# Modulation rows by plain fp32 matmuls on unsplit blocks, spread over the first layer

## The chip, the cores and the metric

One core of one Trainium2 chip runs the whole program. The metric is the device time of one execution in microseconds, the median of several runs. Work on the core is shared by TensorE (PE, matmuls; PEld is its weight load), VectorE (DVE), ScalarE (ACT), GpSimd (POOL) and SyncE (SP); in this kernel SP only issues weight loads and POOL mostly issues the small transfers.

## The reference, cut to what matters

A two-layer diffusion backbone on 128 context and 256 latent tokens, model width 1024, all in fp32. Every sub-block is steered by "adaLN" rows, which come from one vector-matrix product per layer and conditioning vector:

```python
def _adaln(cvec, w, b):
    m = (jax.nn.silu(cvec) @ w + b).reshape(-1, 1, 6 * D_MODEL)
    return jnp.split(m, 6, axis=-1)
...
mp = _adaln(c_ctx, mod_w[i], mod_b[i])
ms = _adaln(c, mod_w[i], mod_b[i])
hp = _modulate(_rmsnorm(xp, norm1_g[i]), mp[0], mp[1])   # shift, scale
... # attention || retention, output projection
xp = xp + mp[2] * op                                      # gate
hp = _modulate(_rmsnorm(xp, norm2_g[i]), mp[3], mp[4])
... # dense SwiGLU (layer 0) or top-2-of-8 experts (layer 1)
xp = xp + mp[5] * fp
```

`mod_w` is 2 x 1024 x 6144 in fp32, 50 MB, multiplied by two vectors only. Layer 0 has a combined input projection (1024 to 2816), windowed attention beside chunkwise retention, an output projection and a SwiGLU; layer 1 has a neighbourhood attention and the experts.

## The kernel before, in words

All large products are made at near-fp32 accuracy out of three fp32r matmuls. A weight block of 128 x 1024 fp32 (512 KB) is loaded by SP into one of `RAW = 6` buffers `rawb`. ACT copies it to `whi` (rounded to fp32r, `conv_hi`, L467), DVE computes `wlo = raw - whi` (`conv_lo`, L472), both in `HL = 3` slots, and TensorE multiplies high by high, high by low and low by high (`mm3`, L522, L525, L526). The blocks of all dense stages have one running number b. SP may reload the raw buffer of b once `lo_done` counts its conversion; ACT may overwrite the slot of b once `pe_used` counts the matmuls of b - 3. The helper `Ahead` lets ACT and DVE convert up to three blocks ahead of TensorE.

The modulation rows go the same way. The two conditioning vectors, after silu and split in high and low, are four stationary columns `cs4` (padded to 128), and each mod block is 2 x 128 rows by 512 columns, moving in four matmuls (L1318 and L1320 in a loop for layer 0, L880 and L882 in `mod1` for layer 1). Twelve chunks of four blocks make the 6144 columns of one layer. Results, four rows of 512, are copied by ACT to `mst` or `mst1` (L1690, L1443), stored by POOL to a scratch in DRAM (L724, L712), and loaded back as rows of `mrow` (`norm_mods`, L718). There DVE multiplies the scale rows by the norm's weight (`scale_rows`, L1760), ACT and DVE split `mrow` into high and low (`split_rows`, L1418, L1764), and TensorE broadcasts the rows to 128 partitions by a matmul with a selector matrix `sel_r` (`rows_bc`, L829; `norm_bc`, and `norm_gate` for the gates). DVE applies them to x (L1778, L1784), TensorE transposes the result (`turn_in`, L861), ACT and DVE split it into `hT_hi` and `hT_lo` (L1424, L1792).

Order of the work, the same on every engine: all 48 mod blocks of layer 0; 8 mod blocks of layer 1; norm 0; the input projection, 22 blocks, with two mod blocks of layer 1 behind each of the first 20 (`MOD_PER`, `mod_behind`); retention, whose matmuls are small plain fp32 ones in eight steps j (L1024, L1036, L1051, L1058, L1059); attention of layer 0 in 24 units n of one head and one token tile (scores L954, transposes L964, values L986, preparation of keys and queries per pair of heads in `prep`, L926 and L933); output projection (8 blocks); norm 1; SwiGLU; norm 2; layer 1's projection, attention, output; norm 3; the experts. Each engine's program is written out by hand, and semaphores tie them together.

In the experts, tokens beyond 128 of one expert are computed from the raw blocks in plain fp32: `oF` and `oT` are 128 x 32 stationary tiles, and four column groups of 32 output rows each take a quarter of the columns (L1235, L1254).

## Time and profile before

| | |
|---|---|
| runs of the kernel before | 2031.91, 2034.63, 2095.38 us, median 2034.63 |
| profiled execution | 2029.53 us, its span 2027.9 us |
| mean granted TensorE clock | 0.915 of full speed |
| busy TensorE | 1842.5 us (91%), 9817 matmul records |
| busy VectorE | 1291.8 us (64%) |
| busy ScalarE | 1088.9 us (54%) |
| moved by DMA | 416.61 MB, mean 205 GB/s |

The page cuts the span into 40 slices of 50.7 us. The first six, in which the mod blocks are loaded, run at 174 to 331 GB/s; the granted clock is near half in slices 7 and 8 (retention and attention of layer 0). A matmul's busy time overlaps that of its neighbour, because it is pipelined, so the distance between the starts of two matmuls tells more than the duration of one. A plain fp32 matmul leaves two records in this trace, an fp32r matmul or a transpose one.

### The profile page before, as it was taken

To read this page: it belongs to the slowest core of one execution; us is meant where nothing else is said; L and a number is where in the kernel's file an instruction comes from. 1 tells how busy PE (TensorE), PEld (TensorE's weight loads), DVE (VectorE), ACT (ScalarE), POOL (GpSimd) and SP (SyncE) were. 2 spreads that over 40 slices of the span, in tenths; PEclk is the share of its full clock that TensorE was granted. 3 is DMA by queue.
4 is the path that set the end of the run, shared out by engine and by line. 5 is a ranking of instruction groups with operands and counts; after the bars stand their busy time and mean duration, and the time that the engine had idled before them with its cause. 6 is when DMAs were issued, how large, how long until landed. Compare 5 with 4: busy or idle time off the path is not lost.

```text
span 2027.9 us, 27794 instructions
## 1 busy us (share of the span) xinstructions
PE 1842.5 (91%) x9817; PEld 1453.8 (72%) x9818; DVE 1291.8 (64%) x1599; ACT 1088.9 (54%) x1493; POOL 154.4 (8%) x225
## 2 busy tenths in 40 slices
PE   4868889999999999999869989999999999999992
PEld 2546677677888877867657868877877777778781
DVE  3764565554434344356537647679898989898985
ACT  3755552433333233356316546567777777777771
POOL 3010010000000004043020000000000000000001
PEclk7879995588999998999859989999999999999996
DMA  8956650022444435422315766789999999999971
GB/s 273 331 174 223 226 184 11 0 86 83 124 124 125 125 107 143 125 68 49 115 53 202 256 245 219 253 314 337 337 337 327 338 325 334 340 334 325 339 267 37
DMA packets 199740, 416.61 MB, mean 205 GB/s; under 512 B 17436, under 2 KB 36948, under 8 KB 199632
## 3 DMA queue, kind: packets, MB, share of 16 engines
q1 hardware_dynamic: 188928, 394.31, 56.8%
q0 software_dynamic: 10704, 20.86, 3.7%
q8 instruction: 67, 1.10, 0.2%
q14 instruction: 41, 0.34, 0.0%
HBM read 415.00 MB, written 5.90 MB: 208 GB/s over the span
## 4 chain that ended last, share of the span: by engine, by line
PE 76%; DVE 11%; ACT 5%; issue 3%; DMA 3%; POOL 0%; SPq 0%; ACTq 0%; DVEq 0%; POOLq 0%
PE ps L522 20%; PE ps L526 19%; PE ps L525 19%; PE ps L954 3%; DVE wlo L495 3%; DMA rawb<-in_mod_w 2%; PE ps L1235 2%; ACT whi L467 2%; PE ps L986 2%; DVE wlo L472 2%; PE ps L964 2%; ACT whi L491 2%; PE ps L1183 1%; PE ps L1254 1%; DVE h L1778 1%
## 5 line engine op out<-in xcount | busy, mean ns | idle before, releaser
L472 DVE TENSOR_TENSOR wlo<-rawb,whi 128x1024 fp32r<-128x1024 f32 x224 | 271.9, 1234 | 344.1 <-ACT whi L467 342.9
L467 ACT ACTIVATE whi<-rawb 128x1024 fp32r<-128x1024 f32 x224 | 231.8, 1055 | 352.2 <-PE ps L526 319.3
L495 DVE TENSOR_TENSOR wlo<-rawb,whi 128x1024 fp32r<-128x1024 f32 x288 | 349.0, 1223 | 111.2 <-ACT whi L491 107.9
L491 ACT ACTIVATE whi<-rawb 128x1024 fp32r<-128x1024 f32 x288 | 304.6, 1060 | 141.1 <-PE ps L526 140.4
L495 DVE TENSOR_TENSOR wlo<-rawx,whi 128x1024 fp32r<-128x1024 f32 x240 | 291.1, 1223 | 56.7 <-ACT whi L491 53.1
L491 ACT ACTIVATE whi<-rawx 128x1024 fp32r<-128x1024 f32 x240 | 254.7, 1061 | 112.8 <-PE ps L526 111.9
L522 PE MATMUL ps<-whi,eT_hi 128*128 128x512 f32 (+1 forms) x768 | 301.7, 393 | 3.8 <-DVE wlo L495 1.9
L525 PE MATMUL ps<-wlo,eT_hi 128*128 128x512 f32 (+1 forms) x768 | 291.1, 379 | 0.0
L526 PE MATMUL ps<-whi,eT_lo 128*128 128x512 f32 (+1 forms) x768 | 291.1, 379 | 0.0
L522 PE MATMUL ps<-whi,hT_hi 128*128 128x512 f32 (+1 forms) x672 | 261.1, 388 | 20.9 <-DVE wlo L472 17.1
L525 PE MATMUL ps<-wlo,hT_hi 128*128 128x512 f32 (+1 forms) x672 | 256.8, 382 | 0.0
L526 PE MATMUL ps<-whi,hT_lo 128*128 128x512 f32 (+1 forms) x672 | 256.7, 382 | 0.0
L522 PEld LDWEIGHTS ps<-whi,eT_hi 128*128 128x128 f32 x768 | 149.1, 194 | 51.2 <-DVE wlo L495 23.8
L526 PEld LDWEIGHTS ps<-whi,eT_lo 128*128 128x128 f32 x768 | 148.9, 194 | 27.2
L522 PEld LDWEIGHTS ps<-whi,hT_hi 128*128 128x128 f32 x672 | 128.2, 191 | 54.8 <-DVE wlo L472 24.6
L525 PEld LDWEIGHTS ps<-wlo,eT_hi 128*128 128x128 f32 x768 | 149.5, 195 | 22.0
L526 PEld LDWEIGHTS ps<-whi,hT_lo 128*128 128x128 f32 x672 | 128.2, 191 | 24.7
L525 PEld LDWEIGHTS ps<-wlo,hT_hi 128*128 128x128 f32 x672 | 128.4, 191 | 22.9
L522 PE MATMUL ps<-whi,eF_hi 128*128 128x512 f32 x352 | 143.7, 408 | 0.0
L526 PE MATMUL ps<-whi,eF_lo 128*128 128x512 f32 x352 | 139.0, 395 | 0.0
L525 PE MATMUL ps<-wlo,eF_hi 128*128 128x512 f32 x352 | 138.8, 394 | 0.0
L522 PEld LDWEIGHTS ps<-whi,eF_hi 128*128 128x128 f32 x352 | 66.2, 188 | 21.7 <-issue 4.5
(311 smaller groups left out, 2430.9 us busy)
## 6 DMA issues: line engine op xcount, KB each, us to landing
rawb<-in_od_moe_w_gu SPq DMA_DIRECT2D x192, 512.0 KB, 5.4
rawx<-in_od_moe_w_gu SPq DMA_DIRECT2D x160, 512.0 KB, 5.3
rawb<-in_mod_w SPq DMA_DIRECT2D x96, 512.0 KB, 5.2
rawb<-in_od_moe_w_down SPq DMA_DIRECT2D x96, 512.0 KB, 5.1
rawx<-in_od_moe_w_down SPq DMA_DIRECT2D x80, 512.0 KB, 5.4
rawb<-in_ev_ffn_w_gu SPq DMA_DIRECT2D x44, 512.0 KB, 3.7
rawb<-in_od_w_qkv SPq DMA_DIRECT2D x24, 512.0 KB, 3.6
rawb<-in_ev_w_in SPq DMA_DIRECT2D x22, 512.0 KB, 3.8
```

The source lines that it names most:

```text
L467: nc.scalar.activation(whi[:, r, :], rawb[:, s, :], ACT.Copy).then_inc(hi_done, 1)
L472: nc.vector.tensor_tensor(wlo[:, r, :], rawb[:, s, :], whi[:, r, :].bitcast(F32), ALU.subtract).then_inc(lo_done, 1)
L491: nc.scalar.activation(whi[:, moe_slot(i), :], moe_raw(j), ACT.Copy).then_inc(hi_done, 1)
L495: nc.vector.tensor_tensor(wlo[:, moe_slot(i), :], moe_raw(i % EB), whi[:, moe_slot(i), :].bitcast(F32), ALU.subtract).then_inc(lo_done, 1)
L522: first_mm = nc.tensor.matmul(out, l_hi, r_hi, start=start, stop=False)
L525: nc.tensor.matmul(out, l_hi, r_lo, start=False, stop=False)
L526: return nc.tensor.matmul(out, l_lo, r_hi, start=False, stop=stop)
L954: nc.tensor.matmul(ps[:, g % 2, 0:hi - lo], qT[r, i % 2, t * P:(t + 1) * P], kT[r, sl, lo:hi], start=True, stop=True).then_inc(at_s, 1)
L964: mm = nc.tensor.transpose(ps[:, 2 + g % 2, c * P:(c + 1) * P], s_p[:, g % 2, c * P:(c + 1) * P], ident)
L986: mm = nc.tensor.matmul(ps[:, 6 + m % 2, DH * u:DH * (u + 1)], s_pT[:, g % 2, c * P:(c + 1) * P], v, start=(c == 0), stop=(c == len(vs) - 1))
L1183: mm = nc.tensor.transpose(ps[:, 6 + s % 2, c * P:(c + 1) * P], eg[:, c * P:(c + 1) * P], ident)
L1235: mm = nc.tensor.matmul(ps[q * OV:(q + 1) * OV, 2 + g, 0:P], oT[:, k, :], moe_raw(j0 + k // rows)[:, c:c + P], start=(k == 0), stop=(k == ...
```

## The change

The modulation product is done without splitting. The two vectors, silu applied, stand in `csz`, 128 x 32 per k, columns 2 to 31 zero, plain fp32. A mod block j is now 128 rows (one k) by the 1024 columns of one of six parts; it is read straight from `rawb` in four fp32 matmuls of 256 columns, each in its own column group of 32 (`mod_mm`). Eight blocks make one of `MODS = 12` parts q. ACT copies a part to `mst` (128 x 256, `mod_take`), POOL stores it and later loads two rows of each group back into `mrow`.

Only parts 0 and 1 (shift and scale of layer 0's first norm) are computed ahead of norm 0. Parts 2 to 5 go behind the first 16 blocks of the input projection, two blocks each; part 6 into retention, one block behind each step; parts 7 to 11 into attention of layer 0, two blocks behind each of 20 units. The gate of layer 0's first sub-block is therefore broadcast during the output projection (`gate_first`), not in norm 0. SP's loads follow one list `SEQ` of mod and weight blocks; a raw buffer is free again when `mod_used` (mod blocks) or `lo_done` (weights) counts it. `whi` and `wlo` hold weight blocks only. Layer 0's `prep` uses one PSUM bank for keys and queries, as bank 4 now takes mod parts 6 to 11. The statistics of norm 0 are computed before the mod parts are taken.

```diff
+MODS, MOD_PER = 12, 2
+B_OUT0 = IN_BLOCKS
+MOD_AFTER = {}
+for _j in range(2 * KD, 6 * KD):
+    MOD_AFTER.setdefault((_j - 2 * KD) // MOD_PER, []).append(_j)
+SEQ = [("m", _j) for _j in range(2 * KD)] + [("w", _b) for _b in range(HL)]
+for _b in range(IN_BLOCKS - HL):
+    SEQ += [("w", _b + HL)] + [("m", _j) for _j in MOD_AFTER.get(_b, ())]
+SEQ += [("m", _j) for _j in range(6 * KD, 7 * KD)] + [("w", B_OUT0 + _b) for _b in range(HL)]
+SEQ += [("m", _j) for _j in range(7 * KD, MODS * KD)] + [("w", _b) for _b in range(B_OUT0 + HL, B_MOE)]
+MOD_IN_ATT = {n: (7 * KD + 2 * i, 7 * KD + 2 * i + 1) for i, n in
+              enumerate(n for s in range(2, 23, 5) for n in range(s, s + 4))}
...
+            for p, (kind, i) in enumerate(SEQ):
+                if p >= RAW:
+                    was, n = SEQ[p - RAW]
+                    sp.wait_ge(*((mod_used, n + 1) if was == "m" else (lo_done, n + 1 + RAW)))
...
+            def mod_store(q):
+                pool.wait_ge(mod_ev, q + 1)
+                if q:
+                    pool.wait_ge(mod_out, 16 * q)
+                pool.dma_start(mods[q], mst[:, q % 2, :]).then_inc(mod_out, 16)
...
+            def gate_first(b):
+                kind = b - B_OUT0
+                if kind not in (0, 1):
+                    return
+                if kind:
+                    pe.wait_ge(gate_ev, 1)
+                else:
+                    pe.wait_ge(mr_l, 2)
+                for half in range(2):
+                    mm = rows_bc(6 + half, 64, 4 + kind, half, 7)
+                mm.then_inc(gate_ps, 1)
...
-            def mod1(b):
-                c, i = b // SB, b % SB
-                pe.wait_ge(lo_done, N_MOD1[b] + 1 + RAW)
...
-                for kk in range(2):
-                    k = 2 * i + kk
-                    nc.tensor.matmul(ps[:, mod_bank(c), :], cs4[:, 4 * k:4 * k + P], wblk(whi, N_MOD1[b], 512)[:, kk, :],
-                                     start=(k == 0), stop=False)
-                    mm = nc.tensor.matmul(ps[:, mod_bank(c), :], cs4[:, 4 * k:4 * k + P],
-                                          wblk(wlo, N_MOD1[b], 512)[:, kk, :], start=False, stop=(k == KD - 1))
-                mm.then_inc(pe_used, 1)
+            def mod_mm(j):
+                q, k = divmod(j, KD)
+                if k == 0 and q == 6:
+                    pe.wait_ge(up_ev, 1)
+                elif k == 0 and q > 3:
+                    pe.wait_ge(mod_ev, q if q > 6 else q - 1)
+                pe.wait_ge(*landed("m", j))
+                for g in range(4):
+                    mm = nc.tensor.matmul(ps[32 * g:32 * (g + 1), mod_bank(q), 0:2 * P], csz[:, k, :],
+                                          rawb[:, slot_at("m", j), g * 2 * P:(g + 1) * 2 * P], start=(k == 0),
+                                          stop=(k == KD - 1))
+                mm.then_inc(mod_used, 1)
...
             def prep(lay, i):
-                kb, qb = (6, 7) if lay and i == 0 else (4, 5)
+                kb, qb = (6, 7) if lay and i == 0 else (4, 5) if lay else (5, 5)
+                if not lay:
+                    if i:
+                        pe.wait_ge(at_qT, i)
+                    else:
+                        pe.wait_ge(gn_c, 1)
...
+                    if lay == 0:
+                        pe.wait_ge(at_kT, ki + 1)
...
+                    if lay == 0:
+                        for j in MOD_IN_ATT.get(n, ()):
+                            mod_mm(j)
...
+            def mod_take(q):
+                act.wait_ge(mod_used, KD * (q + 1))
+                if q > 1:
+                    act.wait_ge(mod_out, 16 * (q - 1))
+                nc.scalar.activation(mst[:, q % 2, :], ps[:, mod_bank(q), 0:2 * P], ACT.Copy).then_inc(mod_ev, 1)
...
+            norm_stats(0)
+            for q in range(2):
+                mod_take(q)
             split_rows(0)
-            norm(0, 0)
-            dense(IN_CH, 0, proj0, tables)
+            ahead = Ahead(act, conv_hi, 0)
+            ahead.to(HL)
+            turn_in(0)
+            dense(IN_CH, 0, proj0, tables, limit=B_OUT0)
```

## Rows read from the trace of the kernel before

**Rows 1.** The page: engines on the chain that ended last; GB/s of its slices
```profile
PE 76%; DVE 11%; ACT 5%; issue 3%; DMA 3%; POOL 0%; SPq 0%; ACTq 0%; DVEq 0%; POOLq 0%
GB/s 273 331 174 223 226 184 11 0 86 83 124 124 125 125 107 143 125 68 49 115 53 202 256 245 219 253 314 337 337 337 327 338 325 334 340 334 325 339 267 37
```

**Rows 2.** Stages: PE, PEld, DVE, ACT, POOL busy, clock, DMA share, GB/s
```profile
0.00:140.60 140.60, 86.46 (x274) 55.91 (x275) 85.89 (x89) 78.44 (x94) 24.49 (x49) 0.81 0.82 277
140.60:295.00 154.40, 137.23 (x593) 107.30 (x592) 81.38 (x85) 85.16 (x119) 5.19 (x10) 0.98 0.63 205
295.00:338.00 43.00, 39.79 (x259) 34.93 (x259) 16.27 (x37) 9.62 (x20) 3.65 (x6) 0.69 0.08 21
338.00:410.00 72.00, 70.37 (x230) 48.10 (x228) 43.58 (x138) 31.66 (x93) 0.00 (x0) 0.50 0.03 8
...
878.00:959.00 81.00, 78.98 (x472) 56.20 (x472) 52.75 (x139) 55.10 (x160) 38.22 (x47) 1.00 0.22 47
```

**Rows 3.** Instructions in order of time, TensorE, input projection: start, duration, line
```profile
162.93 0.51 PE L522 MATMUL ps<-whi,hT_hi 128*128 128x512 f32 x1 [0.60 <-DVE wlo L472]
...
167.16 0.39 PE L880 MATMUL ps<-whi,cs 128*128 128x512 f32 x1
...
169.88 0.47 PE L522 MATMUL ps<-whi,hT_hi 128*128 128x512 f32 x1 [0.71 <-DVE wlo L472]
```

**Rows 4.** The same view, TensorE in the experts, 1163 to 1167 us
```profile
1163.97 0.40 PE L526 MATMUL ps<-whi,eF_lo 128*128 128x512 f32 x1
1164.30 1.93 PE L1254 MATMUL ps<-rawb,oF 128*32 128x256 f32 x32
1166.16 0.50 PE L522 MATMUL ps<-whi,eF_hi 128*128 128x512 f32 x1
```

**Rows 5.** The chain in order of time, retention and attention: start, us, what
```profile
303.90 0.72 PE ps L1036 x6
...
310.20 0.72 PE ps L1036 x6
...
320.32 1.39 PE ps L1036 x6
...
325.45 1.39 PE ps L1036 x6
...
359.22 1.57 PE ps L954 x2
```

**Rows 6.** In order of time, ACT and POOL, early front
```profile
33.73 1.06 ACT L467 ACTIVATE whi<-rawb 128x1024 fp32r<-128x1024 f32 x1 [0.27 <-DMA rawb<-in_mod_w]
...
33.29 1.51 POOL L704 DMA_DIRECT2D mrow<-in_mod_b  x3
```

**Rows 7.** In order of time, POOL, DVE, ACT, TensorE; one row of DMA issues
```profile
104.36 0.52 POOL L724 DMA_DIRECT2D mods_scratch<-mst  x1 [18.69 <-ACT mst L1690]
108.34 1.54 POOL L718 DMA_DIRECT2D mrow<-mods_scratch  x3 [3.45 <-DMA mods_scratch<-mst]
...
mrow<-mods_scratch POOLq DMA_DIRECT2D x6, 16.0 KB, 3.2
...
119.30 1.22 DVE L1760 TENSOR_TENSOR mrow<-mrow,gbc 6x1024 f32<-6x1024 f32 x1
...
121.09 1.04 ACT L1418 ACTIVATE mr_hi<-mrow 128x1024 fp32r<-128x1024 f32 x1
122.16 1.23 DVE L1764 TENSOR_TENSOR mr_lo<-mrow,mr_hi 128x1024 fp32r<-128x1024 f32 x1 [1.64 <-ACT mr_hi L1418]
...
127.49 1.28 DVE L1778 SCALAR_TENSOR_TENSOR h<-x,st,ps 128x1024 f32<-128x1024 f32 x1
...
138.56 0.79 PE L829 MATMUL ps<-mr_hi,sel_r 6*128 6x512 f32 x1 [1.38 <-DVE hT_lo L1792]
```

**Rows 8.** Stretches around the turn after attention, columns as in rows 2
```profile
410.70:414.10 3.40, 3.40 (x18) 3.40 (x17) 2.01 (x3) 2.19 (x4) 0.00 (x0) 0.50 0.00 0
414.20:417.60 3.40, 1.83 (x11) 1.39 (x10) 3.20 (x4) 1.18 (x3) 0.00 (x0) 1.00 0.00 0
```

## What I predict before the changed kernel is run

> **What bounds the kernel now.** I first read the page. TensorE is 76% of the chain that ended last, and the DMA engines reach at most 340 GB/s in any slice [rows 1]. An average over the whole run says little here, so I cut the run into stages at the first and last matmul of each [rows 2]. The first 140.6 us produce modulation rows and the first normalization: TensorE is busy for 86 us of them and idle for the rest. The input projection takes 154.4 us, with the DMAs at 205 GB/s. Retention takes 43 us, attention of layer 0 takes 72 us at a granted clock of 0.50 (the 1.2 GHz level), and attention of layer 1, which is twice as long (48 units against 24), takes only 81 us at 1.00 (2.4 GHz). Everything after the output projection of layer 0 is untouched by the change.
>
> Inside the projection, TensorE does one w_in block and then two mod blocks. The block that starts at 162.93 runs to 167.16 (4.23 us), the two mod blocks need about 1.9 us, and the next block starts only at 169.88, after a wait for wlo [rows 3]: a period of 6.95 us. The reason is in the code. There are three whi/wlo slots for w and mod blocks alike, so the next w block can be converted only when the previous w block has left its slot, and the two mod matmul groups are shorter than that conversion.
>
> **The price of a new mod block.** The routed layer already has the new form: plain fp32 matmuls, 128 rows by 32 columns, 256 columns moving, four column groups, on raw blocks. Each such matmul leaves two records. Thirty-two records, which are 16 matmuls or four blocks, run from 1164.30 to 1166.16 [rows 4]: 1.86 us, or 0.465 us a block at full clock; at half clock I take twice that, 0.93. Around the group 0.10 us is lost going in (0.33 between starts instead of 0.23) and I take as much coming out. So a pair costs 0.93 + 0.2 = 1.14 us, and a lone block 0.68. Before, a pair of blocks cost 1.9 us on TensorE plus one conversion pass per block on ACT and one on DVE. The lower bound is 0.465 without any switch. The upper bound is four matmuls one after another: the nearest row is a score matmul of 384 columns, 1.57 us at half clock for its two records [rows 5], so 256 columns cost 1.05 us at half clock and 0.52 at full, and a block 2.1 us at full clock. I take the low value, because its row has this very form.
>
> The Trainium skill (TensorEngine Tiling, Key Properties) says that changing the tiling mode drains TensorE. If every one of the 88 switches (16 in the projection, 8 in retention, 20 in attention, in and out) cost a whole 0.39 us matmul over its start distance of 0.23, the sum would be 14 us for switching where the rows above give 9, and the forecast 5 us higher.
>
> **Part 1, the front.** Of 56 mod blocks that ran before the first normalization, 16 stay (shift and scale of layer 0); none is converted. What ends last now is the arrival of these 16. The seventh block was converted at 33.73, already paced by its DMA, and POOL comes to the end of its early queue at 34.8 [rows 6]; both stay. A block is 0.524 MB; at 340 GB/s it takes 1.55 us, but four to six of the later blocks will be in flight or landed by then, since a raw slot is now free as soon as TensorE has read it. I put the sixteenth at 43 us (41 if all of the ring is in by 33; 47.7 if nine blocks follow the seventh one by one). Behind it stands a chain that was hidden by the eight early blocks of layer 1 and is now exposed, its steps taken from [rows 7]: matmuls and the copy to mst 1.2; the store from 104.36 to the issue of the load at 108.34, 4.0; two load issues 1.0 and landing 3.2; scaling 1.22, high part 1.04, low part 1.23 with their hand-overs, 3.7 (the copy of sel moves ahead of the wait). That is 56.1. Then norm: before, the low part ended at 123.39, h began at 127.49 and the last transposed low part released TensorE at 138.56. The statistics are now early, but three conversions stand in DVE's queue ahead of h (last wlo about 3.3 us after the low part), so h begins about 3.5 us after the low part instead of 4.1, and the projection starts at 56.1 + 3.5 + 11.1 = 71, rounded up to 72 for the semaphore delays left out. The gate matmuls (138.56 to 140.6) go to the output projection. The gain is 140.6 - 72 = 68.6 us; bounds 62 to 72.
>
> **Part 2, the projection.** 22 w blocks, 32 mod blocks behind the first 16 of them (before: 40 split ones). The wlo stall goes, because mod blocks no longer take whi/wlo slots: conversion of block b+3 now has two whole blocks of cover. Period 4.1 + 1.14 = 5.25, so 16 x 5.25 + 6 x 4.1 = 108.6, and 2 us for the first blocks at half clock: 111 against 154.4, a gain of 43.4. What is late next is the loads: three blocks (1.57 MB) each 5.25 us are 300 GB/s, under the 340 seen. In the ring of six the load of w(b+5) waits for the conversion of b+3, and the mod loads behind it on SP wait with it; from there (2.3 us of conversion, about 6.7 us to land three, 5.25 us of matmuls) the loop closes in 14.3 us for three periods, 4.8 each, less than 5.25. The margin is small, which is a rival below. The four copies to mst (ACT, 256 columns each) and the stores on POOL lie beside the matmuls.
>
> **Part 3, retention.** One block after each of the eight steps. TensorE hardly waits there, so all of it is on the path: 8 x 0.68 = 5.4 at full clock, 9 at half. A step took 3.15 us at full clock (303.90 to 310.20, two steps) and 5.13 later (320.32 to 325.45, one step) [rows 5]. The dense pieces may keep the clock up for a step or two more, 2 us each. I take +3 (bounds -8, the clock holds throughout, and +9).
>
> **Part 4, attention of layer 0.** Forty blocks in pairs behind 20 of the 24 units. At full clock a unit costs 81/48 = 1.69 us, preparations included; at half clock 72/24 = 3.0 [rows 2]. The preparations now share one PSUM bank and wait for ACT's copy of the keys, twice, and the first one waits for the group norm: +3. The question is the clock. The stage is entered at 0.50 after a DVE-only gap, as before, and the old mix never raised it in 72 us, while layer 1, entered at 1.00, held it with the same mix. Now 1.9 us of full-array work stand in each unit of 4.9 us. The clock rose at about 414 after nothing but transposes back to back [rows 8], so short dense work is enough to raise it. I expect it to rise within about three units: 24 x 1.69 + 20 x 1.14 + 3 + 2 x 1.3 (units before it) + 3 x 2.0 = 75, +3. Loads: 37 blocks x 1.55 = 57 us, covered.
>
> The Trainium skill (TensorE: Matmul & The Clock Gate, Part 4: PE-mode transpose) says that transposes do not count as activity of the engine for the clock. By that rule a third of the attention mix would not help, and the rival at 1960 would be the likelier. The trace speaks against it: 0.50 while only transposes ran, 1.00 right behind them.
>
> **Part 5, turn and output projection.** Of the 24 transposes 18 filled 3.4 us at half clock [rows 8]; at full clock the 4.5 us of all become 2.2: -2.3, say -2.4. Two gate groups of four matmuls at 0.23, +1.9. The rest of these rows (DMAs to mrow, six late stores) is hidden behind 30 us of projection and the norm. -0.5.
>
> **Sum.** -68.6 - 43.4 + 3 + 3 - 0.5 = -106.5, against the profiled execution's 2029.5 (span 2027.9 and 1.6 around it): **1923 us**. The median of the runs is 2034.6, 5 us above; I keep 1923.
>
> **Rivals.**
> (a) *The clock stays at 1.2 GHz through attention.* For: 72 us without a rise. Against: the dense pieces. Then 72 + 40 x 0.93 + 3 = 112 instead of 75, and the transposes stay slow: +39, **1962**. Chance 0.27.
> (b) *The loads become the bound in the projection*: mod blocks sit behind w loads on SP and in the same ring. For: 300 GB/s asked. Against: whole slices ran at 334 to 340 GB/s in the experts, and the loop closes. If the period stays 6.95: 16 x 1.7 = +27, **1950**. Chance 0.10.
> (c) *The column groups do not run side by side* when they stand alone on four new matmuls with a fresh 32-column load: 2.1 us a block, 96 x 1.6 = +154, **2077**, slower than before. It decides from (106.5 / 96) + 0.49, about 1.6 us a block. Against: the rows of the same form. Chance 0.02.
> (d) *The change does not do what it says*, that is, the store and load round trip or POOL's early queue holds the first norm until the old time: all 68 us of the front would be lost, **1991**, about 2% faster. Against: POOL is free at 34.8. Chance 0.02.
> My forecast has the remaining 0.59. Its own range is 1905 to 1942 (front -4/+6, retention -11/+6, attention -5/+8, projection +6).
>
> **Range.** 1903 to 1966 takes in (a) and (b). About 2% (41 us) is what a measurement tells from no change: faster 0.95, same 0.03, slower 0.02.
>
> **What would show it.** First projection matmul near 72; a projection period near 5.25 without waits for wlo; mod groups of 0.47 us a block at 1.00; in attention the granted clock at 1.00 after three or four units; the stage from keys to the last value near 75. A clock of 0.50 throughout means (a), waits for rawb in the projection mean (b), groups of 2 us mean (c).

## The result and the profile after

The changed kernel took 2016.01 us in the median of seven runs (2006.81 to 2023.53). The kernel before, run beside it, took 2037.26 us in the median of seven (2031.91 to 2095.59). The ratio is 0.991, 95% interval 0.988 to 0.994. I had forecast 1923 us, with 1903 to 1966 as the range and 0.95 for a gain of over 2%. It is a gain of about 1%, outside the range.

The cause lies in the spread, so it is told here: the runs of the kernel before stand in two groups, 2028 to 2040 us and 2092 to 2106 us, and the ratio leaves the slower group out.

The page of the changed kernel: the granted clock in 40 slices of 50.3 us, the GB/s of the slices, and the engines on the chain that ended last.

```profile
PEclk7799579799999799555859989999999999999996
GB/s 295 147 288 193 76 248 253 70 126 126 123 124 126 107 139 112 32 11 32 116 54 236 255 217 243 259 312 332 347 337 329 336 327 339 327 331 342 335 264 38
PE 80%; DVE 9%; DMA 4%; ACT 3%; issue 3%; POOL 0%; SPq 0%; DVEq 0%; ACTq 0%; POOLq 0%
```

The clock is low in slices 5 and 6 (retention and attention of layer 0), as it was before a little later. It is also low in slices 17 to 19, at 5, 5 and 5, which hold almost nothing but attention of layer 1. The stages of the changed kernel, columns as in [rows 2]; the rows are the front, the input projection, its end to the first scores, attention of layer 0 up to the first output-projection matmul, from there to the SwiGLU, layer 1's projection, and layer 1's attention up to its output projection:

```profile
0.00:76.30 76.30, 24.24 (x170) 10.82 (x171) 18.43 (x30) 15.27 (x25) 20.60 (x41) 0.66 0.71 238
76.30:191.30 115.00, 113.85 (x688) 83.34 (x688) 33.27 (x43) 39.98 (x69) 4.41 (x8) 0.97 0.70 238
191.30:254.00 62.70, 57.64 (x323) 44.76 (x322) 17.34 (x39) 9.59 (x21) 4.22 (x7) 0.56 0.25 76
254.00:332.40 78.40, 72.04 (x574) 41.57 (x574) 48.49 (x144) 38.48 (x106) 2.72 (x5) 0.85 0.83 296
332.40:387.70 55.30, 49.26 (x200) 37.11 (x200) 32.41 (x37) 20.72 (x27) 3.67 (x7) 0.86 0.28 89
695.10:796.50 101.40, 101.40 (x442) 83.57 (x441) 30.58 (x23) 34.42 (x41) 15.08 (x19) 0.97 0.44 128
796.50:951.80 155.30, 150.99 (x506) 106.39 (x505) 60.74 (x151) 60.31 (x169) 38.35 (x47) 0.52 0.11 27
```

The same last stage in the kernel before, 875.7 to 965.2:

```profile
875.70:965.20 89.50, 83.85 (x506) 59.86 (x505) 57.95 (x151) 60.28 (x169) 38.22 (x47) 1.00 0.21 48
```

Both rows hold 506 TensorE records and within 3 us the same DVE, ACT and POOL work. One is at 0.52 and the other at 1.00, and that is 155.3 us against 89.5. Placed side by side by the first matmul of each stage:

| stage begins (us) | before | changed | gain so far |
|---|---|---|---|
| input projection | 140.6 | 76.3 | 64.3 |
| (its end) | 294.7 | 191.3 | 103.4 |
| scores of layer 0 | 337.5 | 254.0 | 83.5 |
| output projection of layer 0 | 416.4 | 332.4 | 84.0 |
| SwiGLU | 468.0 | 387.7 | 80.3 |
| scores of layer 1 | 875.7 | 796.5 | 79.2 |
| output projection of layer 1 | 965.2 | 951.8 | 13.4 |
| end of the span | 2027.9 | 2014.0 | 13.9 |

The change gained 80 us in layer 0, and 66 of them went in one stage that the diff doesn't touch. How that stage loses its clock, first at its start, TensorE in order of time (start, duration, line, what; in brackets the idle time before):

```profile
796.15 0.39 PE L527 MATMUL ps<-whi,hT_lo 128*128 128x512 f32 x1
796.47 0.49 PE L957 MATMUL ps<-kT,qT 64*128 64x128 f32 x4
797.34 0.91 PE L957 MATMUL ps<-kT,qT 64*128 64x384 f32 x2 [0.38 <-DVE s_sc L1897]
800.06 0.44 PE L967 MATMUL ps<-keep,s_p 128*128 128x128 f32 x1 [1.81 <-issue]
```

Then the two stretches at its start and two at its end:

```profile
795.80:799.20 3.40, 2.07 (x10) 0.87 (x8) 1.06 (x4) 2.61 (x4) 0.00 (x0) 1.00 0.43 157
799.20:802.60 3.40, 2.54 (x7) 1.28 (x7) 1.92 (x3) 3.03 (x10) 0.00 (x0) 0.51 0.00 0
945.90:949.30 3.40, 3.40 (x18) 3.40 (x17) 1.65 (x3) 1.83 (x4) 0.00 (x0) 0.50 0.00 0
949.40:952.80 3.40, 1.83 (x12) 1.44 (x11) 3.21 (x5) 1.54 (x3) 0.00 (x0) 1.00 0.00 0
```

TensorE leaves a dense projection and then waits 1.81 us, because in `attention(1)` the program waits for the last evictions of the projection (L1001 `gm_ev`), behind the third unit's scores and ahead of the first unit's transposes. The clock goes to 0.50 (1.2 GHz) inside that idle time, at 799.2, and comes back only at 949.4, in the transposes behind the stage. The kernel before has the same idle at the same place in its program and kept 1.00:

```profile
879.32 0.30 PE L964 MATMUL ps<-keep,s_p 128*128 128x128 f32 x1 [1.81 <-issue]
```

### The profile page after: what moved, and what is told of

Same layout as the page of the kernel before. It is cut to its first block, busy times and chain, and to the rows that moved or that the text cites. A ratio compares the mean times of both kernels' runs of the same rounds, so it can differ in the third digit from the quotient of the medians.

```text
span 2014.0 us, 27918 instructions
## 1 busy us (share of the span) xinstructions
PE 1838.7 (91%) x10201; PEld 1429.4 (71%) x10202; DVE 1180.8 (59%) x1500; ACT 986.6 (49%) x1385; POOL 153.5 (8%) x221
## 4 chain that ended last, share of the span: by engine, by line
PE 80%; DVE 9%; DMA 4%; ACT 3%; issue 3%; POOL 0%; SPq 0%; DVEq 0%; ACTq 0%; POOLq 0%
PE ps L523 20%; PE ps L527 19%; PE ps L526 19%; PE ps L957 4%; DVE wlo L496 3%; PE ps L989 3%; DMA rawb<-in_mod_w 2%; PE ps L1243 2%; PE ps L877 2%; PE ps L967 2%; ACT whi L492 2%; PE ps L1191 1%; PE ps L1262 1%; DVE h L1777 1%; DVE acc L2059 1%
## 5 line engine op out<-in xcount | busy, mean ns | idle before, releaser
L496 DVE TENSOR_TENSOR wlo<-rawb,whi 128x1024 fp32r<-128x1024 f32 x288 | 349.2, 1223 | 111.1 <-ACT whi L492 107.8
L492 ACT ACTIVATE whi<-rawb 128x1024 fp32r<-128x1024 f32 x288 | 304.7, 1061 | 141.2 <-PE ps L527 140.5
L473 DVE TENSOR_TENSOR wlo<-rawb,whi 128x1024 fp32r<-128x1024 f32 x128 | 158.7, 1243 | 309.8 <-ACT whi L468 309.0
L468 ACT ACTIVATE whi<-rawb 128x1024 fp32r<-128x1024 f32 x128 | 135.1, 1058 | 321.8 <-PE ps L527 321.6
L523 PEld LDWEIGHTS ps<-whi,hT_hi 128*128 128x128 f32 x672 | 128.5, 191 | 39.1 <-issue 8.6
L877 PE MATMUL ps<-rawb,csz 128*32 128x256 f32 x768 | 66.8, 463 | 24.9 <-DMA rawb<-in_mod_w 24.5
```

Source lines behind the costliest of these rows:

```text
L468: nc.scalar.activation(whi[:, r, :], rawb[:, slot_at("w", b), :], ACT.Copy).then_inc(hi_done, 1)
L473: nc.vector.tensor_tensor(wlo[:, r, :], rawb[:, slot_at("w", b), :], whi[:, r, :].bitcast(F32), ALU.subtract).then_inc(lo_done, 1)
L492: nc.scalar.activation(whi[:, moe_slot(i), :], moe_raw(j), ACT.Copy).then_inc(hi_done, 1)
L496: nc.vector.tensor_tensor(wlo[:, moe_slot(i), :], moe_raw(i % EB), whi[:, moe_slot(i), :].bitcast(F32), ALU.subtract).then_inc(lo_done, 1)
L523: first_mm = nc.tensor.matmul(out, l_hi, r_hi, start=start, stop=False)
L877: mm = nc.tensor.matmul(ps[32 * g:32 * (g + 1), mod_bank(q), 0:2 * P], csz[:, k, :], rawb[:, slot_at("m", j), g * 2 * P:(g + 1) * 2 * P], ...
```

## The experiments

Two theories stood against each other. **Start theory:** whether layer 1's attention keeps the clock is decided by its light moments, above all the idle at its start, and by where they fall; once down, its mix of work never brings the clock back. **Total-work theory:** the changed kernel has more TensorE work packed into layer 0, and pays for it later wherever the idle falls. I call an execution kept when its mean granted clock is 0.911 or more and lost when it is 0.891 or less. Every execution of the two kernels and their fully computed variants is in one of these groups, and each profiled one of the kept group has layer 1's attention at 1.00. All seven executions of the changed kernel above are lost ones, so the ratio of 0.991 sets them against kept ones of the kernel before.

All variants use one helper, whose results nobody reads:

```diff
+            def fill(n, bank, lo=0, hi=3 * P):
+                for _ in range(n):
+                    nc.tensor.matmul(ps[:, bank, lo:hi], hT_hi[:, 0, 0:P], hT_hi[:, 0, 0:hi - lo],
+                                     start=True, stop=True)
```

**e1 and e2: the idle filled behind the scores.** The changed kernel and the kernel before, each with

```diff
+                    if lay and n < 3:
+                        fill((1, 1, 10)[n], 7)
```

> The changed kernel, with 12 extra 384-column fp32r matmuls (results in a free PSUM bank, read by nobody) in TensorE's idle time at the start of attention of layer 1. Theory A (the gain of the first layer is real, about 84 us, and 66 us of it were given back because the clock fell to 0.50 in the lull at the start of layer 1's attention and stayed there for 150 us): the clock stays at 1.00 through that attention, its stage falls from 155 to about 90 us, total 1948 to 1956. Theory B (the longer attention of layer 1 has another cause, such as POOL's queue or loads moved by the change, and the clock only follows): the stage stays above 130 us and the total within 1 per cent of 2016.

> The kernel before with the same 12 extra matmuls at the start of attention of layer 1. Theory A: in the kernel before, the lull is passed at 1.00 in some executions (2032 to 2037) and not in others (2093 to 2096, 3 of 7). With the lull filled every execution is in the faster group: 2030 to 2038, none at 2095. Theory B: two groups as before, and the fill adds at most 1 us.

e1 took 2013.39 us (0.9905 of the kept executions of the kernel before, 0.9856 to 0.9954), four of four lost. e2 took 2066.99 us in the median, two of four lost; its kept two are at 0.9995 (0.9963 to 1.0028). Both missed what was expected. The fill did carry the clock past the start, but not through the stage. e1, with no idle left ahead of the transposes; then from the first scores to the fall, and on:

```profile
798.54 2.00 PE L809 MATMUL ps<-hT_hi 128*128 128x384 f32 x10
800.39 0.27 PE L972 MATMUL ps<-keep,s_p 128*128 128x128 f32 x1
```

```profile
796.10:809.00 12.90, 12.20 (x63) 8.23 (x62) 7.76 (x19) 10.11 (x26) 2.40 (x2) 1.00 0.11 39
809.00:945.50 136.50, 135.91 (x455) 96.89 (x455) 51.43 (x131) 49.11 (x142) 35.96 (x46) 0.50 0.12 28
```

Ten fills were more than the idle held, so all that follows stood 0.68 us later, and the clock fell 13 us in. So the idle at the start isn't the only moment at which this stage can lose the clock; what made it fall there was not found. e2's profile is of a lost execution (2099.47): its clock falls 12.9 us in as well, and the stage takes 151.1 us. No lost execution of the unaltered kernel before was profiled, so that its group near 2096 is the same loss is inferred, from e2 and from its mean clock of 0.879 to 0.890.

**e3 and e4: more fills, and a shift.** e3 is e1 with fills also in the idle moments of retention and of layer 0's attention; e4 is the changed kernel with `fill(10, 3)` ahead of layer 1's projection.

> The changed kernel with extra matmuls in three lulls: start of retention (9), the group-norm gap and start of attention of layer 0 (about 29), start of attention of layer 1 (12). Theory A: retention is entered and kept at 1.00, its stage (end of projection to first score) falls from 62.7 to about 40 us, attention of layer 0 starts at 1.00 and its stage falls from 78 to about 68 us, attention of layer 1 as in the first run: total 1915 to 1930. If the clock falls inside retention all the same (as it did at 311.7 in the kernel before, where nothing stood idle), retention gives back only half: 1930 to 1940. Theory B: within 1 per cent of 2016.

> The changed kernel with 10 extra 384-column matmuls (1.7 us) in the dense stretch before layer 1's projection, which moves the lull of layer 1's attention by 1.7 us against the start of the program and fills nothing. If what decides is only where in time the lull falls (a fixed relation to the start of the execution), all executions leave the slow group: about 1957. If that is random from execution to execution, some executions come at 1957 and some at 2018. If the lull of the changed kernel is deeper than that of the kernel before, all stay at 2018.

e3 took 2015.28 us (0.9909, 0.9873 to 0.9944), e4 2022.5 (0.9938, 0.9886 to 0.9991), all eight executions lost. e3 missed. e4 came out as the last of its three cases, but not for the reason given there: its idle is 1.81 us, as in the kernel before, and not deeper. In e3 the clock fell 15 us into the stretch behind the input projection instead of 7, and again in layer 0's attention from 260.4 to 308.2, so the fills bought nothing there.

**e5: two fills ahead of the first scores** of the changed kernel.

```diff
+            fill(2, 1)
             attention(1)
```

> The changed kernel with two matmuls of 128x384 (0.17 us each at full clock, results unused) ahead of the first scores of the attention of layer 1, so that this stage starts 0.34 us later and is otherwise the same. Timing theory: whether the clock survives the stage depends on where its light moments (the 1.8 us idle at its start, the single-chunk units at each pair of heads) fall; the start moved by 0.34 us brings them where they stood in the kernel before, the granted clock stays 1.00 through the stage, it takes about 89 us in place of 155, and the time is 1945 to 1962. Total-work theory (the changed kernel's extra matmuls earlier cost it the clock later, whatever the place): the clock falls within 15 us of the start as in all 19 executions so far, and the time is 2012 to 2020.

1948.24 us (1941.86 to 1957.66), four of four kept. The total-work theory falls: more work, and 68 us less in the median. But the stage was not simply later. Its start, and its clock:

```profile
789.64 0.39 PE L527 MATMUL ps<-whi,hT_lo 128*128 128x512 f32 x1
789.87 0.51 PE L809 MATMUL ps<-hT_hi 128*128 128x384 f32 x2
790.31 0.49 PE L962 MATMUL ps<-kT,qT 64*128 64x128 f32 x4
793.55 0.30 PE L972 MATMUL ps<-keep,s_p 128*128 128x128 f32 x1 [1.46 <-issue]
```
```profile
790.30:878.00 87.70, 83.83 (x506) 59.86 (x505) 56.55 (x149) 59.91 (x169) 38.33 (x47) 1.00 0.19 47
```

From the last projection matmul to the first transpose it is 3.91 us (789.64 to 793.55), as in the changed kernel (796.15 to 800.06). What ends that wait doesn't move, so the fills took 0.35 us out of the idle and left all that follows in its place.

**e6: eight fills in the same place, in the kernel before.**

> The kernel before with eight such matmuls (1.36 us) ahead of the first scores of the attention of layer 1. Timing theory: the stage now starts at a moment where it can't keep the clock; every execution falls to 1.2 GHz and takes 2095 to 2106, none the 2032 to 2040 that half of the executions of the kernel before take. Total-work theory: 1.4 us more does nothing; the executions stay in two groups, near 2034 and 2097, about half each.

2036.8 us (2032.84 to 2041.39), four of four kept where I expected four lost, while beside it six of seven plain executions of the kernel before were lost. The miss has the same reason: 1.4 us came out of the idle (0.40 left of 1.81) and nothing was shifted. This is what separated a third theory, that only the **length of the idle** decides, from the one that its **place** decides.

**e7: light moments filled throughout**, in the changed kernel: 1, 1 and 7 fills behind the scores of the first three units, and

```diff
+                    if lay and 3 <= n < N and n % 6 < 4:
+                        fill(2, 4)
```

> The changed kernel with unused matmuls of 128x384 in the light moments of layer 1's attention: 1, 1 and 7 behind the scores of its first three units, then 2 behind the scores of the first four units of each six (about 75 in all, 12.8 us if none of it lies in idle time). Timing theory: with its light moments filled the stage keeps 2.4 GHz wherever it starts; it takes 90 to 102 us and the time is 1950 to 1965. If light moments are not what costs the clock, it falls within 15 us of the start as in e1, the stage takes over 155 us, and the time is 2015 to 2035.

1958.28 us (1952.96 to 1967.93), four of four kept, stage 802.4 to 903.1 at 1.00, as the timing theory expected. The fill costs about 11 us and is worth it, but needs much more than e5. It differs from e1 in two ways, the three fills fewer in the third unit, so that they fit into the idle, and the fills of the later units; which of the two saves it was not tried.

**e10 and e11: place against length.** Both are the changed kernel. e10 puts two fills ahead of the last chunk of the projection, so that everything moves by 0.34 us and the idle stays; e11 has e6's eight.

```diff
-            dense(QKV_CH, GM_DONE[1], 4, lambda: prep(1, 0))
+            dense(QKV_CH, GM_DONE[1], 4, lambda: (fill(2, 6), prep(1, 0)))
```

> The changed kernel with the same two unused matmuls as in e5, but ahead of the last chunk of the query-key-value projection, where nothing waits: the last chunk, its evictions and all of layer 1's attention come 0.34 us later, and the idle at the stage's start stays 1.8 us long (in e5 it was shortened to 1.46). Place theory: where the stage's idle falls decides; 0.34 us later it stands as in the kept execution of the kernel before, the clock stays 1.00 in three of four executions or more, and the median is 1945 to 1960. Gap theory: only the length of the idle decides; it is as long as in the changed kernel, the clock falls near its end, and the time is 2012 to 2022.

> The changed kernel with eight unused matmuls of 128x384 ahead of the first scores of layer 1's attention, as in e6: they take 1.4 us out of the idle at its start and leave what follows in its place. Gap theory: the clock stays 1.00 in every execution and the time is 1940 to 1960, as with two. Place theory alone: the first scores stand 1.36 us later against the clock's changes and the outcome is open; a fall within 15 us in some executions, with times of 2010 to 2020 among them.

e11: 1948.78 us (1945.98 to 1959.99; 0.9573, 0.9487 to 0.9658), four of four kept. e10: 1938.33, 1942.53 and 1948.36 kept, 2009.37 and 2023.26 lost, which is neither what the place theory expected nor what the gap theory did. Its profiled execution is a lost one, with the idle at full length:

```profile
790.60 0.49 PE L962 MATMUL ps<-kT,qT 64*128 64x128 f32 x4
794.19 0.30 PE L972 MATMUL ps<-keep,s_p 128*128 128x128 f32 x1 [1.81 <-issue]
```
```profile
790.60:796.30 5.70, 3.51 (x20) 2.06 (x19) 2.69 (x7) 5.51 (x13) 0.00 (x0) 1.00 0.25 84
796.30:943.00 146.70, 146.12 (x489) 103.79 (x486) 56.88 (x143) 54.02 (x157) 38.34 (x47) 0.50 0.11 26
```

In the profiles of e5 and e10 the last rise of the clock before the stage and the first scores are 96.7 us apart (693.6 to 790.31; 693.9 to 790.60). With 1.46 us of idle the clock stayed, with 1.81 it fell. That is one execution of each, and e10 itself was kept three times of five, so the two fills of e5 (four of four) show the effect of the length less firmly than eight fills do. There the profiles of e6, e11, e14 and e15, with 0.40 us of idle, have the first scores 97.6 to 97.8 us behind the rise, and all four kept the clock; e4's profile, at 97.9 us with the full 1.81 us, lost it, as did all four executions of e4.

The place seems to count too. Three kept of five at full length in e10, against one of twelve for the unshifted kernel, says so weakly. The profiles fit it: of the eight with the full 1.81 us, the two kept ones have the first scores 96.4 and 96.6 us behind the last rise (the kernel before, and e12 below), the six lost ones 96.2 (the changed kernel, e8, e9), 96.7 (e10, e13) and 97.9 us (e4). This order was read from the traces afterwards; no run tested it.

**e13, e14 and e15: the three side by side on one chip**, the changed kernel unaltered, the changed kernel with e11's fills, the kernel before with e6's.

> The changed kernel once more, unaltered, beside the next two on one chip. Gap and place theory: layer 1's attention loses the clock in nearly all executions, 2007 to 2025 us each.

> The changed kernel with the eight unused matmuls in the idle at the start of layer 1's attention (as in e11), beside the unaltered one and the kernel before with the same eight. Every execution keeps the clock there: 1943 to 1960 us. If that was the chip or chance, some executions at 2007 to 2025.

> The kernel before with the same eight matmuls in the same idle (as in e6): every execution 2031 to 2042 us, none near 2096. With the clock of layer 1's attention so held in both kernels, the change is worth this minus e14: 84 to 94 us, against 21 us between the medians of the plain kernels.

| | median us | executions | kept |
|---|---|---|---|
| kernel before | 2037.28 | 2027.77 to 2038.87 and 2096.24 to 2102.84 | 10 of 16 |
| e15, before, idle filled | 2036.47 | 2029.04 to 2039.97 | 11 of 11 |
| e13, changed | 2014.04 | 1943.85; 2009.90 to 2018.05 | 1 of 5 |
| e14, changed, idle filled | 1948.91 | 1945.20 to 1960.00 | 5 of 5 |

e14 against the kept executions of the kernel before is 0.9607 (0.9569 to 0.9645), e15 is 1.0004 (0.9988 to 1.0020). The one kept execution of the unaltered changed kernel shows that the program can go either way. e14's start, where 0.40 us of the idle is left:

```profile
793.78 1.58 PE L809 MATMUL ps<-hT_hi 128*128 128x384 f32 x8
795.29 0.49 PE L962 MATMUL ps<-kT,qT 64*128 64x128 f32 x4
797.46 0.30 PE L972 MATMUL ps<-keep,s_p 128*128 128x128 f32 x1 [0.40 <-issue]
```
```profile
795.30:883.40 88.10, 83.83 (x507) 59.87 (x506) 58.01 (x152) 59.02 (x167) 38.35 (x47) 1.00 0.18 43
```

Over all runs, with the idle filled from in front of the scores, the clock was kept 13 of 13 times in the changed kernel (e5, e11, e14) against 1 of 12, and 15 of 15 in the kernel before (e6, e15) against 21 of 46. With the clock held in both, the change is worth 2036.47 - 1948.91 = **87.6 us** (the two profiled executions are 80 us apart).

**e8, e9 and e12: what the blocks in retention and attention cost, and whether they lift the clock.** e8 and e9 issue one of the four column groups (e8 in layer 0's attention, e9 in retention); e12 does so in both and with 4 columns in place of 256.

```diff
-                for g in range(4):
+                for g in range(4 if j < 7 * KD else 1):
```

e9 has `range(1 if q == 6 else 4)` there, and e12

```diff
+                w, n = (2 * P, 4) if q < 6 else (4, 1)
+                for g in range(n):
```

with w in place of 2 * P in the columns.

> The changed kernel with one of four column groups in each modulation block of parts 7 to 11, those that stand in the attention of layer 0 (three quarters of these parts' sums are left out). Theory that the modulation matmuls raise the clock there: with a quarter of their instructions the clock, down at the stage's start, stays 0.50 for most of the stage as in the kernel before, and the stage takes 78 to 90 us since the instructions left out give back only part of it. Rival, that the clock rises by itself: it rises 13 to 20 us after the stage's start as in the changed kernel, and the stage takes 60 to 68 us.

> The changed kernel with one of four column groups in the eight modulation blocks that stand in the retention (three quarters of part 6's sums are left out; the blocks of the attention of layer 0 stay whole). Theory that the blocks cost their own time there: each block at half clock is 1.08 us of TensorE in the changed kernel, so eight of them lose about 5 to 6 us and the stretch from the end of the input projection to the first scores of the attention goes from 62.7 (54 to 63 in the variants) to 49 to 55 us, with the clock falling 5 to 15 us after the projection's end all the same. Theory that the blocks bring the fall of the clock: with a quarter of them the clock falls only some 15 us after the projection or not at all, as before the change, and the stretch takes 43 to 47 us.

> The changed kernel with the modulation blocks of the retention and of layer 0's attention (parts 6 to 11) cut to one column group of four columns each, so that their loads, waits and order stay and nearly all their TensorE time goes (these parts' sums are left out). The run with one of four groups in the retention showed a block as long as with four (1.06 us against 1.08) and a step with a block of 6.31 us, against 5.14 without one in the variant of the kernel before. If that time is the four column tiles running side by side, the step now falls to 5.2 to 5.5 us at half clock and the stretch from the projection's end to the first scores to 45 to 50 us with the clock falling 7 to 15 us in. If a block's cost is the entry of another tile mode or the wait for its load, whatever its columns, the step stays at 6.0 to 6.3 us and the stretch at 56 to 59 us. In layer 0's attention the clock, if the blocks are what lifts it, stays 0.50 for over 50 of some 72 us; if not, it rises 10 to 20 us after the stage's start as in seven of nine profiles of the changed kernel and its variants.

The sums that these runs leave out change the numbers that reach the experts, and the whole times (3011.57, 3020.26 and 2900.45 us, one execution each) are not compared; only the stages up to layer 1's attention are read. A retention step at half clock from one block to the next, in e9 (one group of 256 columns) and in e12 (one of 4):

```profile
209.69 1.06 PE L877 MATMUL ps<-rawb,csz 128*32 128x256 f32 x2
...
216.00 1.06 PE L877 MATMUL ps<-rawb,csz 128*32 128x256 f32 x2
```
```profile
209.23 0.27 PE L878 MATMUL ps<-rawb,csz 128*32 128x4 f32 x2
...
214.75 0.27 PE L878 MATMUL ps<-rawb,csz 128*32 128x4 f32 x2
```

The same step without a block, in e6:

```profile
316.05 1.59 PE L1041 MATMUL ps<-rqT,rkT 64*128 64x128 f32 x6
...
321.19 1.59 PE L1041 MATMUL ps<-rqT,rkT 64*128 64x128 f32 x6
```

That is 6.31, 5.52 and 5.14 us, and in the changed kernel, with all four groups, the step is 6.34. A block lengthens it by 1.2 us at half clock: 0.8 for its 256 columns, whether one group or four, and 0.4 for being there at all. So e8 and e9 took nothing off TensorE, and both expectations missed: one group costs what four do. For the stretch behind the projection e9 gave 57.4 us and e12 52.4, with the clock falling 13.8 and 12.3 us in. e12's step and stretch lie just above what was expected if the columns cost the time (5.2 to 5.5 and 45 to 50), well below what was expected if they don't.

For layer 0's attention: e8's clock rose 15.7 us in (stage 77.9 us) and e12's only after 89.6 us of its 91.6.

```profile
246.20:261.90 15.70, 13.98 (x34) 5.59 (x34) 12.27 (x28) 8.46 (x20) 0.00 (x0) 0.50 0.47 159
261.90:275.60 13.70, 11.83 (x67) 7.43 (x66) 7.40 (x26) 6.07 (x20) 0.56 (x1) 1.00 0.98 370
```
```profile
241.60:331.20 89.60, 82.65 (x331) 59.06 (x332) 47.51 (x141) 37.93 (x104) 2.72 (x5) 0.50 0.76 259
```

In layer 1, e12 begins its scores at 796.47 us, as the changed kernel does, with the same 1.81 us of idle, and kept the clock (e8 and e9 lost it):

```profile
796.50:886.00 89.50, 83.81 (x507) 59.91 (x506) 58.04 (x152) 60.29 (x169) 38.33 (x47) 1.00 0.19 48
```

## Why the prediction was wrong, step by step

**The step that failed** is the sentence "Everything after the output projection of layer 0 is untouched by the change". Its instructions are untouched; its clock is not. I had 1.00 for layer 1's attention before me in [rows 2] and took it for a property of the stage. It was one of two outcomes, and the runs shown held both: 2095.38 beside 2031.91 and 2034.63. I compared 2029.5 with the median and never asked what the 61 us between the runs were, nor which idle moment of an untouched stage could be worth that. The row of that stage in [rows 2] begins at 878, inside the idle (877.52 to 879.32), so I never had its start in view. The changed kernel arrives with the same 1.81 us of idle and lost the clock 11 times in 12. The cost is +65.8 us, and unused matmuls that fit into the idle, ahead of the first scores, give it back (e5, e11, e14). That much is shown, and with it that the loss hangs on how the stage is entered. That the idle alone causes it is not: e12, the kernel before and others kept the clock with the idle at full length, and e1, e2 and e3, with the idle filled from behind the scores, lost 10 times in 12, later in the stage. Why the unaltered programs differ in how often they lose (11 of 12; 25 of 46, which chance alone would give about once in fifty) is only argued: they reach that idle at slightly different moments against the clock's earlier changes. The distances given under e10 speak for it, and of the shifted programs e10 kept three of five and e4 none of four.

The other terms, measured in the profiled executions against my sum:

**Front: -64.3, predicted -68.6.** POOL's early queue, and the chain behind the last block, in the changed kernel:

```profile
38.00 0.57 POOL L676 DMA_DIRECT2D rpb_scratch<-in_od_rpb  x1 [23.24 <-DMA rpb_scratch<-padrow]
...
49.44 0.56 POOL L695 DMA_DIRECT2D mods_scratch<-mst  x1 [8.75 <-ACT mst L1447]
55.14 1.16 POOL L701 DMA_DIRECT2D mrow<-mods_scratch  x2 [5.15 <-DMA mods_scratch<-mst]
```
```profile
47.61 1.08 PE L877 MATMUL ps<-rawb,csz 128*32 128x256 f32 x8 [1.86 <-DMA rawb<-in_mod_w]
61.40 0.81 PE L809 MATMUL ps<-mr_hi,sel_r 6*128 6x512 f32 x2 [12.71 <-DVE mr_lo L1759]
```
```profile
57.79 1.22 DVE L1755 TENSOR_TENSOR mrow<-mrow,gbc 6x1024 f32<-6x1024 f32 x1 [36.40 <-DMA mrow<-mods_scratch]
...
65.22 1.28 DVE L1777 SCALAR_TENSOR_TENSOR h<-x,st,ps 128x1024 f32<-128x1024 f32 x1 [0.46 <-PE ps L809]
```

POOL's early queue ends at 40.1, not 34.8, but the store at 49.44 comes 8.75 us after that queue is empty, waiting for the rows of the second part, so rival (d) is out. The sixteenth block is done at 48.7, not 43: it is paced by its load to the end, as in my upper case of 47.7. Store to load is 5.7 us (49.44 to 55.14) where [rows 7] had 4.0; from the load to the scaling it is 2.7 (57.79), where I had 4.2. From the scaling to the projection at 76.3 it is 18.5 us, and my sum had 19.6. So the chain behind the sixteenth block is 27.6 us against my 29, and what failed is the arrival, 5.7 us late.

**Projection: -39.1 (154.1 to 115.0), predicted -43.4.** No wait for wlo is left. The pairs of blocks:

```profile
99.48 1.07 PE L877 MATMUL ps<-rawb,csz 128*32 128x256 f32 x16
104.82 1.07 PE L877 MATMUL ps<-rawb,csz 128*32 128x256 f32 x16
...
115.89 0.64 PE L877 MATMUL ps<-rawb,csz 128*32 128x256 f32 x8 [0.30 <-DMA rawb<-in_mod_w]
117.18 0.64 PE L877 MATMUL ps<-rawb,csz 128*32 128x256 f32 x8 [0.66 <-DMA rawb<-in_mod_w]
```

The period is 5.34 us against my 5.25, so a pair comes to 1.24 us on top of a block's 4.1, against 1.14. It is set by TensorE, where before it was the wait for wlo [rows 3]. The two waits for loads shown, 0.96 us, are nearly all that the stage has of them (1.1), so rival (b) is out, and so is (c): a block takes 0.5 us of TensorE at full clock, not 2. The rest is the start, at half clock for 6 us.

**Retention and the way to the scores: +19.9 (42.8 to 62.7), predicted +3.** This is the largest mis-sized term behind the failed step. Eight blocks at the 1.2 us each that e9 and e12 give at half clock, and less before the fall, come to about 9 (an estimate), as my upper bound had it. The first preparation waits 1.8 us for the group norm (0.7 before). The rest goes with the clock: it fell 7.2 us behind the projection's end instead of 17.0. In the changed kernel and its variants the stretch is the shorter the later the clock falls: 62.7 us at 7.2, 57 to 59 at 11.8 to 14.6 (nine profiles), 52.9 at 19.5 (e11). I had taken -8 to +9 as its bounds, with the hope that "dense pieces" keep the clock. They didn't, and an earlier fall was not among my cases. But both profiles compared here are the extremes of their kind. In the other profiles of the kernel before with fills in layer 1 (e2, e6, e15) the clock fell 10.5 to 11.4 us in and the stretch took 47.5 to 48.2 us. Against those the stretch loses some 10 to 11 us, and the rest of the 19.9 is the luck of the two executions; that the blocks bring an earlier fall is not shown.

**Attention of layer 0 with the turn behind it: -0.5 (78.9 to 78.4), predicted +3 - 2.4 = +0.6, and the clock does rise.** The changed kernel's first stretches:

```profile
254.00:270.20 16.20, 14.58 (x71) 6.16 (x72) 12.26 (x28) 8.46 (x20) 0.00 (x0) 0.50 0.50 168
270.40:283.60 13.20, 11.33 (x102) 7.31 (x100) 7.40 (x26) 6.12 (x20) 0.56 (x1) 1.00 0.98 356
```

It rose after 16 us instead of 9, and dipped once from 283.8 to 290.7. e12 says that the columns of the blocks do it: without them it stays down for 89.6 us, as it does for over 76 us in the four profiles of the kernel before and its variants, while with them it rose within 59 us in all twelve. e12 is one execution. But it is no steady state: in e4 and e7 the clock rose only after 55 and 58 us, and in e13 it fell again for 31 us (276.2 to 306.9). Over the profiles of the changed kernel and its variants the stage takes 77 us (e5) to 93 us (e7), or 94 in e3 with its own fills. Rival (a) thus happens in part in some executions, and costs up to some 16 us, not 39.

The Trainium skill (TensorE: Matmul & The Clock Gate, Part 4: PE-mode transpose), cited in the prediction against this step, counts transposes as no activity. The stretch from 945.9 shown above is transposes at 0.50, followed by 1.00, so the trace speaks against that rule once more.

**Output projection to the SwiGLU: +3.7 (51.6 to 55.3), predicted +1.9 for the gate matmuls.** The two groups of gate matmuls take about 2 us (at 336.8 and 342.3). The stretch at half clock ahead of the SwiGLU is 15.1 us long against 13.7, which explains less than 1 us more; the remainder stays open.

**The sum.** The misses of these terms are 4.3 + 4.3 + 16.9 - 1.1 + 1.8 = 26.2 us. Added to 1923 they give 1949, and e14, with the clock held, runs 1948.9. That the two agree to a microsecond is luck: some 8 or 9 of the 16.9 us are the two extreme executions, and the profiles of e15 and e14 divide otherwise (front 64.0, projection 37.5, retention -11.4, attention of layer 0 -1.2, all later stages together -8.5, where I had nothing but the 1.9 of the gates). What holds is the size: about 20 to 26 us of mis-sized terms, which my range would have covered, and one missing step of 66.

## What to carry to other kernels

When the runs of a kernel fall in two groups, find out first which stage makes them differ, since a change that touches nothing there can still move the kernel from one group to the other. A stage that stands at full clock in one profile may depend on a microsecond or two of idle at its entry; look for the wait on a dense-to-light boundary, and put work into it: here eight unused matmuls ahead of the first scores, 1.4 us that fit into the 1.8 us of idle, are worth 65 us. Twelve in other places of the same start were worth nothing, so measure several executions of each. The version that beats both kernels is e14, at 1948.9 us; real work in that place, such as the next pair's preparation, was not tried.

## What the runs showed of the hardware that I had not expected

- The same mix of work is stable at both clocks: entered at 1.00, layer 1's attention stays there for 88 us; once it has fallen, it stays at 0.50 for 137 to 150 us, with TensorE busy 146 of 147 us (e10).
- Four column groups of 32 take the time of one: 1.08 and 1.06 us for a block at half clock. A block of 4 columns still takes 0.27 us and lengthens its step by 0.4.
- Unused matmuls can be free or harmful by a microsecond: eight, which fit into the idle, cost nothing in the kernel before (1.0004), and twelve, which pushed the rest 0.68 us later, left the clock to fall 13 us into the stage in the three profiles that have them (e1, e2, e3), and 10 of 12 executions lost.
